# Entry of two retrieval layers: first dots and products ahead of the second tile's norm and queries, and six gather places first

## The chip, the cores and the metric

The kernel runs on one core of one Trainium2 chip. The metric is the device time of one launch in microseconds, as the median of several runs.

## The reference

Two blocks of a transformer work on 256 tokens of width 1024, and a third block (sparse attention, linear attention, mixture of experts) follows. Everything is float32. After its mixer each of the first two blocks runs a product-key retrieval layer, and that is where the change lies. Cut to what matters:

```python
def peer_ffn(h, w_q, sub_keys, down, up):        # h: 256 tokens in blocks of 128
    q = (xb @ w_q).reshape(n, 8, 2, 128)         # 8 heads, 2 halves of a key
    s = einsum('thpk,pnk->thpn', q, sub_keys)    # 128 scores for each half
    s_top, i_top = top_k(s, 16)
    best_s, best_pos = top_k(all 16 x 16 sums, 16)
    idx = ...                                    # 16 experts for each head: 128 picks a token
    gate = softmax(best_s)
    act = gelu(einsum('thkd,td->thk', down[idx], xb))
    return einsum('thk,thkd->td', gate * act, up[idx])

x = x + g1 * mixer(...)
h2 = rms_norm(x, norm2_g) * (1 + sc2) + sh2
x = x + g2 * peer_ffn(h2, ...)
```

Each token picks 128 experts out of 16384. Each expert is a row of 1024 numbers to be dotted with the token and another row of 1024 to be added to the output.

## The kernel before

The tokens are two tiles of 128 (NT), a token to a partition. The two expert rows lie side by side in HBM, 8 KB for an expert. One gather is one indirect DMA issued by POOL (line 676): it brings pick n of all 128 tokens of a tile, 1 MB, into a gather place. A layer has 256 gathers, 128 for each tile. There are eight places (GSLOTS): 0 to 3 lie in the arena, 4 to 7 in two slots of the weight ring that the layer borrows. Places 4 and 5 need the mixer's output weights to be used up (semaphore pout1), places 6 and 7 the first chunk of the query weights, which both tiles use (semaphore pq).

Two picks make a group, here called a round j, of which a layer has 128 (GROUPS). For each round DVE makes two dots, one a gather (down, line 1423), each a fused multiply and sum over 1024 columns. ACT applies gelu and the gate and turns the two results into two diagonal matrices (weigh, lines 885 to 894). PE multiplies these with the second halves of the two gathered rows and accumulates in PSUM (line 2278, "the up product"), and then increments up_used. POOL, which waits for up_used, then issues the gathers that reuse the two places. So a place is taken from the issue of a gather to the end of its round's product.

The picks of the next heads are worked out among all this. PE makes a query step s in four quarters of eight matmuls each (quarter; L1921), then scores(s) (L2231); ACT copies both out (query_out, score_out); DVE runs top-k in 15 steps (top_k) between dots. A step s is a chunk of four key halves for one tile, in the order QUERY; step 0 is done in two half steps (first_query, first_scores), so that head 0's picks come early. The tables QUARTERS and QUERIED say after which rounds j the quarters and scores of steps 3 to 7 stand. All orders are written out by hand, one program for each engine. In layer 0 the order around the entry is this.

- DVE: norm of tile 0, top-k of head 0 (which releases gather 0), residual of tile 1 (add_tile(1)), norm of tile 1 (start(1)), then the dots with top-k steps between them.
- PE: transposes and first query halves of tile 0, last projection of the mixer, step 1 and its scores, transposes of tile 1 (turn(1)), step 2 and its scores, then the rounds.
- ACT: copies for these, then the sum of squares and root of tile 1 (enter(1)), then its copies, then the rounds.
- POOL: gathers 0 to 3, 4 and 5 (pout1), 6 and 7 (pq of step 2), then two after each round.

In layer 1 the norm of tile 1 comes before the top-k of head 0 in both kernels. SP loads the query weights of chunk 3 (wq0_last, wq1_last) once the slot of chunk 1 is free, that is after step 3, and two rows of modulation weights after steps 6 and 7; each of these loads is 2 MB.

Of the kernel before, what the change touches and what calls it, by code (L numbers as in the profile page):

```python
# [22 lines left out]
NT = T // P  # L23
# [7 lines left out]
PICKS = 128  # L31
GSLOTS = 8
# [90 lines left out]


QUERY = [(0, 0), (1, 0), (0, 1), (1, 1), (2, 0), (3, 0), (2, 1), (3, 1)]
QUARTERS = {3 * (i // 2) + i % 2: (3 + i // 4, i % 4) for i in range(20)}
QUERIED = {j: s for j, (s, k) in QUARTERS.items() if k == 3}


def selections(l, m, head=1):  # L130
# [4 lines left out]
PER = 2  # L135
GROUPS = PICKS * NT // PER


def slot_free(l, n):

    return GROUPS * l + (n - GSLOTS) // PER + 1


def operand(tag, n):
# [64 lines left out]
def program(nc, a, out):  # L209

    ctx = ExitStack()
    with ctx:
# [10 lines left out]
        S = Sems()  # L223
# [130 lines left out]
        turn = list(range(RING))  # L354
# [91 lines left out]

        def gslot(l, n):

            k = n % GSLOTS
            if k < 4:  # L450
                return G_arena[:, k]
            return ring[:, lent[l][(k - 4) // 2], 2 * D * (k % 2):2 * D * (k % 2) + 2 * D]

        def wait_gathered(eng, l, n):
            eng.wait_ge(S[f"gathered{n % GSLOTS}"], 16 * ((PICKS * NT * l + n) // GSLOTS + 1))

        g_landed = [S[f"g_landed{i}"] for i in range(2)]

# [17 lines left out]
        place = mo(NT, 34)  # L476
# [179 lines left out]
        @block.gpsimd  # L656
        def _(pool):
            for l in range(2):
                for n in range(PICKS * NT):
                    t, at = n // PICKS, n % PICKS  # L660
                    if n == 0:
                        pool.wait_ge(S["idx_ready"], 9 * l + 1)
                    elif n == HEAD:
                        pool.wait_ge(S["idx_ready"], 9 * l + 2)
                    elif n % (2 * HEAD) == 0:
                        pool.wait_ge(S["idx_ready"], 9 * l + n // (2 * HEAD) + 2)
                    if n >= GSLOTS:
                        if n % PER == 0:
                            pool.wait_ge(S["up_used"], slot_free(l, n))
                    elif n == 4 and l == 0:  # L670
                        pool.wait_ge(S["pout1"], 4)
                    elif n == 6:
                        pool.wait_ge(S["pq"], query_no(l, QUERY.index((0, 1))))
                    elif l and n == 0:
                        pool.wait_ge(S["up_used"], GROUPS * l)
                    pool.indirect_dma_start(  # L676
                        out=gslot(l, n), out_offset=None, in_=a["experts"],
                        in_offset=bass.IndirectOffsetOnAxis(ap=idx_all[:, t, at:at + 1], axis=0)).then_inc(
                        S[f"gathered{n % GSLOTS}"], 16)


        @block.scalar
        def _(act_):
# [142 lines left out]
            def peer(l):  # L826
# [42 lines left out]
                head_out(0)  # L869
                head_out(1)  # L870
                gate_out(0, 0)
                query_out(1)
                score_out(1)
                if l == 0:
                    enter(1)
                turned_out(2)
                turned_out(3)
                query_out(2)
                score_out(2)

                def weigh(j):
                    t, at = PER * j // PICKS, PER * j % PICKS
# [14 lines left out]
                for j in range(GROUPS):  # L897
                    g, i = j // 8, j % 8
                    weigh(j)
                    if j - 1 in QUERIED:  # L900
                        query_out(QUERIED[j - 1])
                    if j - 3 in QUERIED:
                        score_out(QUERIED[j - 3])
                    if j == 4:
                        gate_out(0)
                    if j == 10 or (j % HEAD == 8 and HEAD < j < 7 * HEAD):
                        gate_out(j // HEAD + 1)
                    if i == 5 and g in TOTALS[l]:
                        mod_total_out(TOTALS[l][g])
                    if l == 0 and (g, i) == (11, 0):  # L910
                        act_.wait_ge(S["x_peer"], 1)
                        tile_sum(x, h, 0)
                    if l == 0 and (g, i) == (13, 0):
                        tile_root("n1_1", 0)
# [184 lines left out]
        def _(v):  # L1099
# [257 lines left out]
            def peer(l):  # L1357
                def start(t):
                    v.wait_ge(S["x_mix"], NT * l + t + 1)
                    tile_mean(f"n2_{l}", t)  # L1360
                    tile_norm(f"n2_{l}", t, x, h, mod[:, 4], mod[:, 3])

                add_tile(0, (4, 5) if l == 0 else (0, 1), mod[:, 2], ("pout1", "py_pool")[l], "x_mix")
# [54 lines left out]
                def down(g):  # L1418
                    t, hh = g // 8, g % 8
                    for k in range(HEAD):  # L1420
                        row = gslot(l, HEAD * g + k)[:, 0:D]
                        wait_gathered(v, l, HEAD * g + k)
                        ins = v.scalar_tensor_tensor(out=row, in0=row, scalar=1.0, in1=h[:, t], op0=ALU.mult,  # L1423
                                                     op1=ALU.mult, accum_out=act[:, t, HEAD * hh + k:HEAD * hh + k + 1])
                        if k % PER == PER - 1:
                            ins.then_inc(S["down_used"], 1)
                        n = HEAD * (g % 2) + k
                        if g < 2:
                            if n == 0:
                                gates(0, 0, 1)  # L1430
                            for step in (2 * n, 2 * n + 1):
                                if step < STEPS:
                                    top_k(0, step, 1, 2)
                            if n == 12:
                                gates(0, 1, 2)
                            if 0 <= n - 9 < STEPS:
                                top_k(1, n - 9)
                        elif g < BLOCKS - 2 and n % 4 < 3 and n - n // 4 < STEPS:
                            top_k(g // 2 + 1, n - n // 4)
                        if g < BLOCKS - 2 and n == 24:  # L1440
                            gates(g // 2 + 1)
# [12 lines left out]
                if l == 0:  # L1454
                    v.wait_ge(S["modp"], 4 + ROWS)
                    v.tensor_tensor(mrows1, bank[7][:, :], mbias, ALU.add).then_inc(S["rows_made"], 1)
                    add_tile(1, (2, 3), mod[:, 2], "pout1", "x_mix")
                    start(1)
                for g in range(BLOCKS):
                    down(g)  # L1460
                    if g == SHADOW - 1:
# [449 lines left out]
        def _(pe):  # L1911
# [289 lines left out]
            def peer(l):  # L2201
# [57 lines left out]
                for k in range(4):  # L2259
                    quarter(1, k)  # L2260
                scores(1)
                turn(1)
                for k in range(4):
                    quarter(2, k)
                scores(2)

                for j in range(GROUPS):
                    g, i = j // 8, j % 8
# [6 lines left out]
                    for k in range(PER):  # L2275
                        row = gslot(l, PER * j + k)[:, D:2 * D]
                        for c in range(2):
                            ins = pe.matmul(bank[2 * t + c][:, :], diag[:, PER * (j % 2) + k], row[:, 512 * c:512 * c + 512],  # L2278
                                            start=j % (GROUPS // NT) == 0 and k == 0,
                                            stop=(j + 1) % (GROUPS // NT) == 0 and k == PER - 1, skip_group_check=True)  # L2280
                    ins.then_inc(S["up_used"], 1)
                    if j - 1 in QUERIED:
                        scores(QUERIED[j - 1])
                    if j in QUARTERS:
                        quarter(*QUARTERS[j])
                    if (g, i) == (SHADOW, 7):
                        pe.wait_ge(S["cB"], 5 + l)
                        pe.wait_ge(S["pq_ev"], query_no(l, 7))
# [437 lines left out]
```

## Time and profile before

| | |
|---|---|
| median of 3 runs | 2444.6 us (2443.27 to 2445.58) |
| profiled execution, its own time | 2443.39 us |
| its span, first to last instruction | 2441.5 us |
| mean granted TensorE clock | 0.97 |
| PE busy, share of the span | 2078.7 us, 85% |
| DVE busy | 1158.2 us, 47% |
| 512 gathers | 536.90 MB, 53.3% of the 16 DMA engines' span |

The span is cut into 40 slices of 61 us. The retrieval layers run from about 230 to 925 us and from about 967 to 1640 us. A share of busy time over the whole span says little about an entry that lasts 60 us; windows and timelines of the two entries are needed.

### The profile page before, as it was taken

To read this page: it belongs to the slowest core of one execution; us is meant where nothing else is said; L and a number is where in the kernel's file an instruction comes from. 1 tells how busy PE (TensorE), PEld (TensorE's weight loads), DVE (VectorE), ACT (ScalarE), POOL (GpSimd) and SP (SyncE) were. 2 spreads that over 40 slices of the span, in tenths; PEclk is the share of its full clock that TensorE was granted. 3 is DMA by queue.
4 is the path that set the end of the run, shared out by engine and by line. 5 is a ranking of instruction groups with operands and counts; after the bars stand their busy time and mean duration, and the time that the engine had idled before them with its cause. 6 is when DMAs were issued, how large, how long until landed. Compare 5 with 4: busy or idle time off the path is not lost. (4 is left out here: it accounts for less than half of the span.)

```text
span 2441.5 us, 21439 instructions
## 1 busy us (share of the span) xinstructions
PE 2078.7 (85%) x7589; PEld 987.9 (40%) x7589; DVE 1158.2 (47%) x2844; ACT 647.2 (27%) x1815; POOL 599.2 (25%) x516
## 2 busy tenths in 40 slices
PE   7999899777777778898777777778999899999998
PEld 2455555232323336554223222224445444444443
DVE  2333675666676555675776667443524311111111
ACT  2232333323332322333323333222341110010011
POOL 0000343444444440343444444430000000000000
PEclk8999899999999999999999999999999899999999
DMA  8595799999999994999999999985321479999996
GB/s 351 206 381 219 282 420 421 421 421 419 412 416 417 414 420 172 386 419 421 421 418 419 412 420 421 408 344 229 157 110 57 191 303 427 426 428 427 428 426 266
DMA packets 98909, 864.05 MB, mean 354 GB/s; under 512 B 11352, under 2 KB 11480, under 8 KB 13552
## 3 DMA queue, kind: packets, MB, share of 16 engines
q0 software_dynamic: 73728, 536.90, 53.3%
q1 hardware_dynamic: 25072, 325.75, 32.1%
q8 instruction: 62, 1.02, 0.2%
q14 instruction: 47, 0.39, 0.0%
HBM read 861.56 MB, written 1.05 MB: 353 GB/s over the span
## 5 line engine op out<-in xcount | busy, mean ns | idle before, releaser
L2278 PE MATMUL bank<-ring,arena 128*128 128x512 f32 x1024 | 478.1, 611 | 141.1 <-ACT arena L894 141.0
L2278 PE MATMUL bank<-arena 128*128 128x512 f32 x1024 | 489.2, 623 | 125.8 <-ACT arena L894 125.8
L676 POOL DMA_INDIRECT arena<-in_experts,arena x256 | 299.2, 1169 | 659.3 <-PE bank L2278 332.7
L1423 DVE SCALAR_TENSOR_TENSOR ring<-ring,h 128x1024 f32<-128x1024 f32 x256 | 313.7, 1225 | 266.3 <-DMA ring<-in_experts,arena 265.6
L1423 DVE SCALAR_TENSOR_TENSOR arena<-arena,h 128x1024 f32<-128x1024 f32 x256 | 313.5, 1225 | 208.8 <-DMA arena<-in_experts,arena 207.7
L676 POOL DMA_INDIRECT ring<-in_experts,arena x256 | 299.9, 1171 | 369.3 <-PE bank L2278 301.2
L2278 PEld LDWEIGHTS bank<-ring,arena 128*128 128x128 f32 x1024 | 187.4, 192 | 414.7 <-ACT arena L894 224.4
L2278 PEld LDWEIGHTS bank<-arena 128*128 128x128 f32 x1024 | 191.4, 196 | 402.9 <-ACT arena L894 206.8
L885 ACT ACTIVATE arena<-arena 128x2 f32<-128x2 f32 x256 | 52.0, 203 | 866.0 <-DVE ring L1423 444.2
L1921 PE MATMUL bank<-ring,hT 128*128 128x512 f32 (+2 forms) x608 | 251.8, 571 | 9.2 <-DVE arena L1671 4.8
L2582 PE MATMUL bank<-ring,arena 128*64 128x512 f32 x768 | 223.4, 593 | 2.2 <-ACT arena L1066 1.2
L894 ACT ACTIVATE arena<-const,arena 128x128 f32<-128x128 f32 x512 | 177.6, 394 | 16.6 <-PE bank L2278 8.4
L1921 PEld LDWEIGHTS bank<-ring,hT 128*128 128x128 f32 x608 | 115.6, 193 | 136.5 <-issue 124.4
L1880 DVE TENSOR_TENSOR arena<-arena,bank 128x512 f32<-128x512 f32 x16 | 11.0, 688 | 307.7 <-PE bank L2582 307.7
L1921 PEld LDWEIGHTS bank<-hT,ring 128*128 128x128 f32 x1024 | 125.0, 197 | 25.0 <-issue 22.9
L2582 PEld LDWEIGHTS bank<-ring,arena 128*64 128x64 f32 x768 | 71.7, 137 | 146.2 <-issue 144.8
L1921 PE MATMUL bank<-hT,ring 128*128 128x128 f32 x1024 | 126.2, 280 | 3.1 <-ACT hT L836 3.1
L889 ACT ACTIVATE arena<-arena 128x1 f32<-128x1 f32 x512 | 122.9, 287 | 8.4
L2628 PE MATMUL bank<-ring,arena 128*64 128x512 f32 x256 | 113.3, 595 | 9.1 <-DVE arena L1882 9.1
L2628 PE MATMUL bank<-arena 128*64 128x512 f32 x256 | 113.3, 595 | 0.0
L2582 PE MATMUL bank<-arena 128*64 128x512 f32 x256 | 112.8, 594 | 0.0
L1066 ACT ACTIVATE arena<-bank 128x512 f32<-128x512 f32 x32 | 17.4, 594 | 214.8 <-PE bank L1921 214.8
(434 smaller groups left out, 1713.5 us busy)
## 6 DMA issues: line engine op xcount, KB each, us to landing
ring<-in_w_gate SPq DMA_DIRECT2D x32, 2048.0 KB, 15.0
ring<-in_mod_w SPq DMA_DIRECT2D x24, 2048.0 KB, 11.7
ring<-in_w_up SPq DMA_DIRECT2D x16, 2048.0 KB, 17.0
arena<-in_w_up SPq DMA_DIRECT2D x16, 2048.0 KB, 21.5
ring<-in_w_down SPq DMA_DIRECT2D x16, 2048.0 KB, 11.5
arena<-in_w_down SPq DMA_DIRECT2D x16, 2048.0 KB, 16.0
ring<-in_w_in SPq DMA_DIRECT2D x9, 2048.0 KB, 7.3
ring<-in_peer_w_q SPq DMA_DIRECT2D x8, 2048.0 KB, 12.4
```

The lines of the kernel that those rows point to most:

```text
L676: pool.indirect_dma_start(out=gslot(l, n), out_offset=None, in_=a["experts"], in_offset=bass.IndirectOffsetOnAxis(ap=idx_all[:, t, at:at + ...
L885: link(act_.activation(part, part, ACT.Gelu_apprx_tanh))
L889: ins = act_.activation(act[:, t, k:k + 1], act[:, t, k:k + 1], ACT.Copy, scale=gate[:, t, k:k + 1])
L894: ins = act_.activation(diag[:, PER * (j % 2) + k], ident, ACT.Copy, scale=act[:, t, at + k:at + k + 1])
L1066: act_.activation(xs[:, 4 * half:4 * half + 4].rearrange("p a b -> p (a b)"), bank[half][:, :], ACT.Copy).then_inc(S["x_sel_ev"], 1)
L1423: ins = v.scalar_tensor_tensor(out=row, in0=row, scalar=1.0, in1=h[:, t], op0=ALU.mult, op1=ALU.mult, accum_out=act[:, t, HEAD * hh + k:HE ...
L1880: v.tensor_tensor(hpair.rearrange("p f c -> p (f c)"), flat_sg, bank[3][:, :], ALU.mult).then_inc(S["pair_made"], 1)
L1921: ins = pe.matmul(dst, lhsT, rhs, start=i == 0, stop=i == len(pairs) - 1)
L2278: ins = pe.matmul(bank[2 * t + c][:, :], diag[:, PER * (j % 2) + k], row[:, 512 * c:512 * c + 512], start=j % (GROUPS // NT) == 0 and k == ...
L2582: ins = pe.matmul(bank[2 + j][CAP * k:CAP * k + CAP, :], xs[:, q, CAP * k:CAP * k + CAP], w_k[3 * k + j][:, q], start=q == 0, stop=q == KT ...
L2628: ins = pe.matmul(bank[c][CAP * k:CAP * k + CAP, :], hsel[:, f, CAP * k:CAP * k + CAP], w_k[3 * k + 2][:, f, 512 * c:512 * c + 512], start ...
```

## The change

In layer 0, DVE makes dot 0 right after the residual of tile 1, then the mean for tile 1's norm; the norm itself stands behind dot 1. ACT does tile 1's sum of squares and root ahead of the copy of step 1. In both layers the first up product stands ahead of tile 1's transposes on PE, and step 2 moves into rounds 1 and 2 (two quarters after each product). The quarters of steps 3 to 7 are dealt out again: ten in each 13 rounds from round 3 to round 27, where there were two in each three from round 0 to round 28. The copies on ACT move with them. The first twelve gathers use only places 0 to 5, so gathers 6 to 11 wait for rounds 0 to 2 instead of step 2; gathers 12 and 13 are the first in places 6 and 7 and wait for step 2; from gather 14 on each gather waits for the round that ended eight gathers earlier, as before.

```diff
-QUARTERS = {3 * (i // 2) + i % 2: (3 + i // 4, i % 4) for i in range(20)}
-QUERIED = {j: s for j, (s, k) in QUARTERS.items() if k == 3}
+QUARTERS = {1: [(2, 0), (2, 1)], 2: [(2, 2), (2, 3)]}
+QUARTERS.update({3 + 13 * i // 10: [(3 + i // 4, i % 4)] for i in range(20)})
+QUERIED = {j: parts[-1][0] for j, parts in QUARTERS.items() if parts[-1][1] == 3}
...
+EARLY_SLOTS = 6
+def place_of(n):
+    return n % EARLY_SLOTS if n < 2 * EARLY_SLOTS else (n - EARLY_SLOTS) % GSLOTS
+def users(place, n):
+    return [m for m in range(n) if place_of(m) == place]
 def slot_free(l, n):
-    return GROUPS * l + (n - GSLOTS) // PER + 1
+    return GROUPS * l + users(place_of(n), n)[-1] // PER + 1
...
 # POOL
-                    if n >= GSLOTS:
+                    if users(place_of(n), n):
                         if n % PER == 0:
                             pool.wait_ge(S["up_used"], slot_free(l, n))
                     elif n == 4 and l == 0:
                         pool.wait_ge(S["pout1"], 4)
-                    elif n == 6:
+                    elif n == 2 * EARLY_SLOTS:
                         pool.wait_ge(S["pq"], query_no(l, QUERY.index((0, 1))))
...
 # ACT
                 gate_out(0, 0)
-                query_out(1)
-                score_out(1)
                 if l == 0:
                     enter(1)
-                turned_out(2)
-                turned_out(3)
-                query_out(2)
-                score_out(2)
+                query_out(1)
...
                     weigh(j)
+                    if j == 0:
+                        score_out(1)
+                    if j == 1:
+                        turned_out(2)
+                        turned_out(3)
...
 # DVE
+                        if l == 0 and (g, k) == (0, 0):
+                            tile_mean("n2_0", 1)
+                        if l == 0 and (g, k) == (0, 1):
+                            shifted(1)
...
                     add_tile(1, (2, 3), mod[:, 2], "pout1", "x_mix")
-                    start(1)
...
 # PE
                 scores(1)
-                turn(1)
-                for k in range(4):
-                    quarter(2, k)
-                scores(2)
...
                     ins.then_inc(S["up_used"], 1)
+                    if j == 0:
+                        turn(1)
                     if j - 1 in QUERIED:
                         scores(QUERIED[j - 1])
-                    if j in QUARTERS:
-                        quarter(*QUARTERS[j])
+                    for part in QUARTERS.get(j, ()):
+                        quarter(*part)
```

The first place is PE at the entry of layer 0 in the kernel before, from step 1 and its scores (L2231) to the products of round 3. L2209 is turn(1), L1921 with 128x128 is a query step or one of its quarters (x8), L2278 the up product; two products without anything between them show as x8.

```order
L1921 MATMUL bank<-hT,ring 128x128 x32
L2231 MATMUL bank<-cols,arena 128x128 x4
L2209 MATMUL bank<-const,h 128x128 x8
L1921 MATMUL bank<-hT,ring 128x128 x32
L2231 MATMUL bank<-cols,arena 128x128 x4
L2278 MATMUL bank<-arena 128x512 x4
L1921 MATMUL bank<-hT,ring 128x128 x8
L2278 MATMUL bank<-arena 128x512 x4
L1921 MATMUL bank<-hT,ring 128x128 x8
L2278 MATMUL bank<-ring,arena 128x512 x8
L1921 MATMUL bank<-hT,ring 128x128 x8
L2278 MATMUL bank<-arena 128x512 x4
```

The same place in the changed kernel, where turn(1) is L2230, a query step or a quarter L1942, scores L2252 and the product L2295.

```order
L1942 MATMUL bank<-hT,ring 128x128 x32
L2252 MATMUL bank<-cols,arena 128x128 x4
L2295 MATMUL bank<-arena 128x512 x4
L2230 MATMUL bank<-const,h 128x128 x8
L2295 MATMUL bank<-arena 128x512 x4
L1942 MATMUL bank<-hT,ring 128x128 x16
L2295 MATMUL bank<-ring,arena 128x512 x4
L1942 MATMUL bank<-hT,ring 128x128 x16
L2295 MATMUL bank<-arena 128x512 x4
L2252 MATMUL bank<-cols,arena 128x128 x4
L1942 MATMUL bank<-hT,ring 128x128 x8
L2295 MATMUL bank<-arena 128x512 x4
```

Round 0's product now stands where turn(1) stood, and the 32 matmuls of step 2 follow products 1 and 2 in two halves of 16.

The second place is DVE in layer 0 before the change, from the end of the residual of tile 1 (L1142) to dot 1. L1126 is the mean, L1131 to L1134 the norm of tile 1, L1423 a dot, L1414 to L1416 the gates of head 0, L1157 and L1159 steps of top-k.

```order
L1142 TENSOR_TENSOR x<-x,arena 128x512
L1126 TENSOR_SCALAR stat<-stat 128x1
L1131 RECIPROCAL stat<-stat 128x1
L1132 SCALAR_TENSOR_TENSOR h<-x,stat,arena 128x1024
L1134 TENSOR_TENSOR h<-h,arena 128x1024
L1423 SCALAR_TENSOR_TENSOR arena<-arena,h 128x1024
L1414 TENSOR_REDUCE cols<-arena 128x1
L1415 RECIPROCAL cols<-cols 128x1
L1416 TENSOR_TENSOR arena<-arena,cols 128x16
L1157 MAX cols<-arena 128x8 x2
L1159 MAX_INDEX cols<-cols,arena 128x8 x2
L1423 SCALAR_TENSOR_TENSOR arena<-arena,h 128x1024
```

The same place in the changed kernel: L1157 is the end of the residual, L1441 a dot, L1141 the mean, L1432 to L1434 the gates, L1146 to L1149 the norm.

```order
L1157 TENSOR_TENSOR x<-x,arena 128x512
L1441 SCALAR_TENSOR_TENSOR arena<-arena,h 128x1024
L1141 TENSOR_SCALAR stat<-stat 128x1
L1432 TENSOR_REDUCE cols<-arena 128x1
L1433 RECIPROCAL cols<-cols 128x1
L1434 TENSOR_TENSOR arena<-arena,cols 128x16
L1172 MAX cols<-arena 128x8 x2
L1174 MAX_INDEX cols<-cols,arena 128x8 x2
L1441 SCALAR_TENSOR_TENSOR arena<-arena,h 128x1024
L1146 RECIPROCAL stat<-stat 128x1
L1147 SCALAR_TENSOR_TENSOR h<-x,stat,arena 128x1024
L1149 TENSOR_TENSOR h<-h,arena 128x1024
```

Dot 0 comes first, and the three instructions of the norm come behind dot 1.

The third place is ACT in the changed kernel, layer 0, from the exponential of head 0's gate (L877): L723 and L728 are enter(1), L856 is query_out(1), L895 to L904 one weigh, L870 is score_out(1), L851 the copies of tile 1's transposes. In the kernel before, the two copies of step 1 stood ahead of enter(1), and the copies of the transposes and of step 2 ahead of the first weigh.

```order
L877 ACTIVATE arena<-arena 128x16
L723 ACTIVATE h,stat<-x 128x1024
L728 ACT_TABLE_LOAD
L728 ACTIVATE stat<-stat 128x1
L856 ACTIVATE arena<-bank 128x512
L895 ACT_TABLE_LOAD
L895 ACTIVATE arena<-arena 128x2
L899 ACTIVATE arena<-arena 128x1 x2
L904 ACTIVATE arena<-const,arena 128x128 x2
L870 ACTIVATE arena<-bank 128x512
L895 ACTIVATE arena<-arena 128x2
L899 ACTIVATE arena<-arena 128x1 x2
```

So query_out(1) now waits behind a root that needs DVE's mean, and the first weigh needs neither tile 1's transposes nor step 2.

## Rows read from the trace of the kernel before

Times are microseconds from the start of the span unless a column is marked ns.

**Rows 1.** Windows: stretch, length, busy of each engine, clock, DMA share, GB/s.

```profile
251.50:293.80 42.30, 38.17 (x181) 25.71 (x180) 27.45 (x93) 14.85 (x41) 14.01 (x12) 0.93 0.62 238
293.80:393.80 100.00, 92.93 (x380) 54.35 (x379) 69.63 (x172) 33.94 (x104) 44.08 (x38) 1.00 1.01 421
500.00:900.00 400.00, 309.43 (x679) 122.41 (x679) 259.55 (x588) 126.46 (x418) 186.52 (x158) 0.98 1.01 417
973.00:1014.60 41.60, 37.48 (x183) 24.77 (x183) 31.24 (x104) 14.96 (x41) 14.32 (x14) 0.96 0.94 368
```

**Rows 2.** Timeline of POOL, layer 0: start, length, issue of one gather [idle before].

```profile
229.54 1.07 POOL L676 DMA_INDIRECT arena<-in_experts,arena  x1 [229.09 <-DVE arena L1407]
236.02 0.94 POOL L676 DMA_INDIRECT ring<-in_experts,arena  x1 [0.30 <-issue]
259.88 1.38 POOL L676 DMA_INDIRECT ring<-in_experts,arena  x1 [22.92 <-PE bank L1921]
270.34 1.60 POOL L676 DMA_INDIRECT arena<-in_experts,arena  x1 [7.84 <-PE bank L2278]
284.21 1.31 POOL L676 DMA_INDIRECT ring<-in_experts,arena  x1 [1.00 <-PE bank L2278]
```

**Rows 3.** Line 676, 229 to 237: gathers 0 (the least) to 5 (the most).

```profile
DMA to landing us min/median/max: 9.8/12.4/15.5
```

**Rows 4.** Line 676: 259 to 262 is gathers 6 and 7; 284.1 to 284.3 is gather 14.

```profile
DMA to landing us min/median/max: 6.0/7.1/8.1
DMA to landing us min/median/max: 9.6/9.6/9.6
```

**Rows 5.** Timeline of DVE, layer 0, where line 1423 is a dot.

```profile
233.52 0.74 DVE L1142 TENSOR_TENSOR x<-x,arena 128x512 f32<-128x512 f32 x1
244.91 0.16 DVE L1131 RECIPROCAL stat<-stat 128x1 f32<-128x1 f32 x1 [1.29 <-ACT stat L713]
247.57 1.22 DVE L1423 SCALAR_TENSOR_TENSOR arena<-arena,h 128x1024 f32<-128x1024 f32 x1
250.37 1.23 DVE L1423 SCALAR_TENSOR_TENSOR arena<-arena,h 128x1024 f32<-128x1024 f32 x1
257.09 1.23 DVE L1423 SCALAR_TENSOR_TENSOR ring<-ring,h 128x1024 f32<-128x1024 f32 x1
```

**Rows 6.** Timeline of ACT, layer 0.

```profile
242.22 1.05 ACT L708 ACTIVATE h<-x 128x1024 f32<-128x1024 f32 x1
263.40 0.20 ACT L885 ACTIVATE arena<-arena 128x2 f32<-128x2 f32 x1
```

**Rows 7.** Timeline of PE, layer 0: L2209 transposes, L1921 queries, L2231 scores, L2278 products.

```profile
247.71 1.97 PE L2209 MATMUL bank<-const,h 128*128 128x128 f32 x8 [6.01 <-DVE h L1134]
264.89 5.17 PE L2278 MATMUL bank<-arena 128*128 128x512 f32 x8 [3.44 <-ACT arena L894]
269.90 1.95 PE L1921 MATMUL bank<-hT,ring 128*128 128x128 f32 x16
285.56 3.60 PE L2278 MATMUL bank<-arena 128*128 128x512 f32 x8
288.99 1.95 PE L1921 MATMUL bank<-hT,ring 128*128 128x128 f32 x16
290.78 3.60 PE L2278 MATMUL bank<-arena 128*128 128x512 f32 x8
```

**Rows 8.** Timelines of DVE and POOL, layer 1.

```profile
976.44 1.22 DVE L1423 SCALAR_TENSOR_TENSOR arena<-arena,h 128x1024 f32<-128x1024 f32 x1 [0.61 <-DMA arena<-in_experts,arena]
973.68 1.41 POOL L676 DMA_INDIRECT ring<-in_experts,arena  x1 [0.30 <-issue]
1004.41 0.93 POOL L676 DMA_INDIRECT ring<-in_experts,arena  x1 [1.26 <-PE bank L2278]
```

**Rows 9.** Line 676, layer 1: gathers 0 (least) to 5 (most); gather 14.

```profile
DMA to landing us min/median/max: 5.5/9.8/13.3
DMA to landing us min/median/max: 10.2/10.2/10.2
```

More of the change, by code:

```diff
@@ L447, in gslot @@
         def gslot(l, n):
-            k = n % GSLOTS
+            k = place_of(n)
             if k < 4:
@@ L454, in wait_gathered @@
         def wait_gathered(eng, l, n):
-            eng.wait_ge(S[f"gathered{n % GSLOTS}"], 16 * ((PICKS * NT * l + n) // GSLOTS + 1))
+            k = place_of(n)
+            eng.wait_ge(S[f"gathered{k}"], 16 * (l * len(users(k, PICKS * NT)) + len(users(k, n)) + 1))
         g_landed = [S[f"g_landed{i}"] for i in range(2)]
@@ L678, in _ @@
                         in_offset=bass.IndirectOffsetOnAxis(ap=idx_all[:, t, at:at + 1], axis=0)).then_inc(
-                        S[f"gathered{n % GSLOTS}"], 16)
+                        S[f"gathered{place_of(n)}"], 16)
         @block.scalar
@@ L1360, in start, with shifted @@
                     tile_mean(f"n2_{l}", t)
+                    shifted(t)
+                def shifted(t):
                     tile_norm(f"n2_{l}", t, x, h, mod[:, 4], mod[:, 3])
```

## The prediction

> **What bounds the kernel now.** The windows come first, because a share over the whole span hides an entry of 60 us. In the body of layer 0 (500 to 900 us) the 16 DMA engines are busy 1.01 of the time at 417 GB/s, while PE is busy 309 of 400 us and DVE 260; in the 100 us after the entry they move 421 GB/s, and there PE too is busy for 93 us, which will matter below [rows 1]. So the transfers set the pace: a gather of 1.049 MB every 2.49 us at 421 GB/s, 4.98 us a round. With that, a retrieval layer ends when its last gather has landed, and what can be won in it is the time at its entry in which the DMA engines have nothing to do.
>
> Next come the issues on POOL and their times to landing. Gathers 0 to 5 of layer 0 are issued from 229.54 to 236.02 and land from 239.3 (229.54 + 9.8) to 251.5 (236.02 + 15.5) [rows 2, 3]. Gather 6 is issued only at 259.88, after 22.92 us of waiting for step 2 of the queries, and lands 6.0 us later, at 265.9; gather 7 lands at 269.7 [rows 2, 4]. Gather 14, issued at 284.21, lands at 293.8 [rows 2, 4]. Between 251.5 and 293.8 nine gathers land, which take 9 x 2.49 = 22.4 us; so 19.9 of these 42.3 us are lost to the DMA, and their window shows 238 GB/s [rows 1]. In layer 1 gather 0 lands at 973.0 and gather 14 at 1014.6 (1004.41 + 10.2) [rows 8, 9]: 41.6 us for 14 gathers, 34.9 us, so only 6.7 are lost, and the window shows 368 GB/s [rows 1]. That is the most that each entry can give.
>
> Last, why the gathers are late. DVE ends the residual of tile 1 at 234.3, but dot 0 starts at 247.57 [rows 5], 8 us after gather 0 has landed, because the norm of tile 1 stands in front and waits for ACT. The first product starts at 264.89 [rows 7], 1.49 after its gelu [rows 6], which stood behind the copies of step 2. All six places are held until then.
>
> **The change in layer 0, step by step.** Dot 0 starts when gather 0 is there: 239.5. From dot 0 to dot 1 it was 2.80 us [rows 5]; the mean adds 0.15, so dot 1 runs from 242.4 to 243.7. The norm of tile 1 costs 2.66 on DVE (244.91 to 247.57 [rows 5]) and now stands behind dot 1; the three steps from 250.37 to 257.09 are 2.24 each [rows 5], so dot 2 starts at 247.3, dot 3 ends at 250.8 and dot 5 at 255.3. All six gathers have landed before their dots from dot 2 on. ACT's sum of squares (1.05 [rows 6]) is done by 236; its root waits for DVE's mean behind dot 0, until 241. That is the one wait added: queued behind it on ACT is the copy of step 1, and behind that PE's scores of step 1. They go 1.3 us later; the first weigh needs dot 1 only at 243.7, so this costs nothing. Without that cover it would be the same 1.3 us.
>
> Product 0 starts 1.5 us after dot 1: 245.2. PE's clock was low after a similar pause and the product took 5.0 us to the next piece (264.89 to 269.90), against 3.43 at full speed (285.56 to 288.99) [rows 7]; I take 5.0, so it ends at 250.2. Tile 1's transposes (1.97 after a pause [rows 7]) follow and end before product 1 can start, at 252.3. It ends at 255.7. Half of step 2, two quarters of 1.79 (288.99 to 290.78 [rows 7]), follows until 259.3; product 2 until 262.8; the other half until 266.4; product 3 until 269.8. POOL issues 0.4 us behind the end of a product (269.90 to 270.34 [rows 2, 7]).
>
> So gathers 6 and 7 are issued at 250.6 and land at 256.6 and 260.4: where the DMA has run dry, the first of a pair takes 6.0, and the pair 269.7 - 259.88 = 9.8 [rows 2, 4]. Gathers 8 and 9 are issued at 256.1 and follow at 262.9 and 265.4. Gathers 10 and 11 are issued at 263.2; the DMA is dry for a moment and they land at 269.2 and 273.0. Gathers 12 and 13 (issued 266.8, after step 2) land at 275.5 and 278.0, and gather 14 (issued 270.2) at 280.5. Before it was 293.8: **a lead of 13.3 us**, of 19.9 that were lost. Six places instead of eight cost nothing in this stretch, as before gathers 6 and 7 came later than any round would have allowed.
>
> **Does the lead hold?** From round 3 PE has 3.43 for each product, 1.79 x 10/13 for quarters, and some 0.9 for scores once in five rounds: 3.43 + 1.38 + 0.18 = 4.99 us a round, against the DMA's 4.98. Before it was two quarters in three rounds, 4.80. PE starts round 4 at 272.5 (round 3's end, scores, a quarter), some 4 us after its dots allow (gather 9 at 265.4 + 1.3 + 1.5 = 268.2). That backlog neither grows nor shrinks, and the DMA has six gathers (14.9 us) in the queue to cover it: landing, dot, weigh, product, issue and start take 1.3 + 1.5 + 3.4 + 0.4 + 3.5 = 10.1, so 4.8 us are to spare. It is tight, but each 2 MB load of SP in this stretch gives PE 5 us more. I take no loss; the bound is in the rivals.
>
> **Layer 1.** Its norm of tile 1 is not moved. Gather 1's dot ends at 977.7 [rows 8], so product 0 starts at 979.2 instead of 985.08, after a pause of 8.6 us in which step 2 used to run: PE has nothing to fill it now. Here are the two ends. At full speed product 0 ends at 982.6, product 1 (dot 3 ended at 983.3) at 988.2, step 2 and product 2 at 995.2, product 3 at 1002.2, and gather 14 lands at 1012.8: a gain of 1.8. If product 0 and the transposes run at 1.2 GHz all through (7.0 and 2.0 us), gathers 6 and 7 come after the six first ones have landed (987.0 = 973.68 + 13.3 [rows 8, 9]), and gather 14 lands at about 1016.6: a loss of 2. The product before, after a pause of 3.4 us, lay between; I take the middle, **0**.
>
> **Sum.** 13.3 + 0 = 13.3 us. The profiled execution took 2443.39, which gives 2430.1; the median is 1.2 above it, so 2431.3. The chip's other work is the same in amount, and the layer's later parts all hang on its last gather.
>
> **Two rules of the Trainium skill.** A gather that finds the DMA dry landed 6.0 us after its issue [rows 4]. The page "DMA: Bandwidth & Descriptors", section "Anatomy of one DMA — SWDGE (gpsimd) path", puts a fixed cost of about 2.0 us beside the bytes over 436 GB/s: by it 1.049 MB would be there after an estimated 4.4 us, and the holes ahead of gathers 6 and 10 would shrink by 1.6 us each, for some 2428. The trace doesn't agree, so the row stands. The other speaks against the change: "TensorE: Matmul & The Clock Gate", section "Loop structure matters more than you think", warns that a wait for DMA between matmuls sends the array back to half clock. The rows show that clock in the product at 264.89; the rival on the clock below is priced from them.
>
> **The rivals.** (1) *The clock stays low.* With product 0 at 7.0 us and the transposes at 2.0 in layer 0, product 1 starts at 254.2 and all that follows 1.9 later; with the loss of 2 in layer 1 the gain is 9.4: 2435.2. For it: a pause in both layers. Against: in layer 0 PE's pauses are short, two of about 2 us. (2) *The other side: the rounds become PE's.* A product that starts after a wait, with a quarter behind it, may take more than 4.98 + its share; the records themselves read 3.60 and 1.95 [rows 7], that is 5.3 to 5.4 a round with 10/13 quarters and the scores, if nothing overlapped. 0.35 to 0.45 us a round for 25 rounds in both layers is 17.5 to 22.5 us, more than the lead: 2449 to 2454. It decides from a mean round of 5.25 us (13.3/50 above 4.98), and makes the kernel slower by over 0.2% from 5.35. Against: starts 3.43 and 1.79 apart, and SP's loads. Half of it, a lead worn down by 7 us, gives 2438. (3) *The change does nothing*, because the layer doesn't end with its transfers, or gathers 0 to 5 land later for a reason outside. Then 2444. Against: 1.01 for 400 us [rows 1]. (4) *Quick restarts and a full clock in both entries*: 13.3 + 1.8 + some 2: 2427.5.
>
> **How the numbers follow.** Forecast (2428.5 to 2433.5) 0.60, rival 4 0.10, rival 1 0.12, rival 2 in its mild form 0.08 and in its strong form 0.04, rival 3 0.06. The range from 2426 to 2438.5 leaves out the strong form, most of rival 3 and the edge of the others, under 2 in 10. A measurement of this kernel tells about 0.2%, 4.9 us: faster is all below 2439.7, 0.89; the same 0.07; slower 0.04.
>
> **What the profile after would show.** Dot 0 near 239.5; product 0 near 245; gather 6 issued at 250 to 252 after waiting for a product and no longer for a query; gathers 10 and 11 near 263; gather 14 landed near 280 (layer 0) and within 2 us of its old place from gather 0 (layer 1); DMA share 1.0 from 283 to the end of the layer. Wrong would be a window between 285 and 400 with the DMA share below 0.97 and PE without pauses (rival 2), a product 0 that takes 7 us (rival 1), or a first dot that waits past 242.

## The result, and the profile after

The changed kernel takes 2429.98 us (median of 5 runs, 2428.41 to 2432.18) against 2443.27 of the kernel before (5 runs, 2442.17 to 2445.58): ratio 0.9946, 95% interval 0.9932 to 0.9961, so 13.3 us less. The forecast was 2431.3 in 2426.0 to 2438.5, faster. The profiled execution is the slowest of the five, 2432.18 us, with a span of 2430.4.

The windows first: stretch, length, busy time of each engine, clock, DMA share, GB/s. They answer to [rows 1]: the entry of layer 0 from the landing of gather 5 to that of gather 14, the 100 us behind it, the body of layer 0, and layer 1 from gather 0 to gather 14.

```profile
254.20:284.80 30.60, 30.60 (x162) 20.99 (x161) 22.10 (x74) 12.22 (x34) 15.12 (x13) 1.00 0.90 341
284.80:384.80 100.00, 96.27 (x416) 58.70 (x415) 69.45 (x171) 34.49 (x104) 39.54 (x38) 0.98 1.01 421
500.00:900.00 400.00, 307.37 (x677) 121.13 (x676) 259.67 (x589) 126.82 (x420) 187.91 (x158) 0.99 1.01 416
964.70:1004.20 39.50, 33.92 (x158) 22.00 (x159) 31.25 (x104) 14.69 (x43) 15.34 (x14) 0.88 0.96 385
```

The body is the same as before (DMA share 1.01, 416 GB/s), so the transfers still set the pace. The entry of layer 0 lasts 30.6 us where it lasted 42.3.

POOL's issues in layer 0, which answer to [rows 2]: start, length of an issue, and what it waited for.

```profile
232.29 1.08 POOL L691 DMA_INDIRECT arena<-in_experts,arena  x1 [231.84 <-DVE arena L1425]
238.76 0.94 POOL L691 DMA_INDIRECT ring<-in_experts,arena  x1 [0.30 <-issue]
254.68 1.64 POOL L691 DMA_INDIRECT arena<-in_experts,arena  x1 [14.98 <-PE bank L2295]
258.99 0.94 POOL L691 DMA_INDIRECT arena<-in_experts,arena  x1 [0.54 <-PE bank L2295]
265.99 1.69 POOL L691 DMA_INDIRECT ring<-in_experts,arena  x1 [4.83 <-PE bank L2295]
269.56 0.94 POOL L691 DMA_INDIRECT ring<-in_experts,arena  x1 [0.45 <-PE bank L1942]
273.00 0.94 POOL L691 DMA_INDIRECT arena<-in_experts,arena  x1 [1.25 <-PE bank L2295]
```

Gather 6 waits for a product (L2295), no longer for a query. Everything is some 2.75 us later than before up to gather 0 (232.29 against 229.54), though nothing was changed ahead of it; in the thirteen profiles of this study gather 0 is issued between 226.4 and 232.3. So times are read from the issue of gather 0 on: gather 6 after 22.4 us (30.3 before), gather 14 after 40.7 (54.7 before).

How long the issues took to land: gathers 0 to 5 (the least is gather 0, the most gather 5), gathers 6 and 7, 8 and 9, 10 and 11, and gather 14, which answers to [rows 3, 4].

```profile
DMA to landing us min/median/max: 9.7/12.4/15.4
DMA to landing us min/median/max: 7.0/7.3/7.7
DMA to landing us min/median/max: 8.0/8.6/9.3
DMA to landing us min/median/max: 7.6/8.0/8.3
DMA to landing us min/median/max: 11.8/11.8/11.8
```

Gather 5 lands at 254.2 and gather 14 at 284.8. From the issue of gather 0 that is 52.5 us, against 64.3 before: 11.8 us won.

DVE in layer 0, dots (L1441), residual (L1157), mean (L1141) and the first piece of the norm (L1146), which answer to [rows 5].

```profile
236.27 0.73 DVE L1157 TENSOR_TENSOR x<-x,arena 128x512 f32<-128x512 f32 x1
242.03 1.22 DVE L1441 SCALAR_TENSOR_TENSOR arena<-arena,h 128x1024 f32<-128x1024 f32 x1 [5.03 <-DMA arena<-in_experts,arena]
243.18 0.15 DVE L1141 TENSOR_SCALAR stat<-stat 128x1 f32<-128x1 f32 x1
244.91 1.23 DVE L1441 SCALAR_TENSOR_TENSOR arena<-arena,h 128x1024 f32<-128x1024 f32 x1
246.06 0.16 DVE L1146 RECIPROCAL stat<-stat 128x1 f32<-128x1 f32 x1
249.87 1.23 DVE L1441 SCALAR_TENSOR_TENSOR arena<-arena,h 128x1024 f32<-128x1024 f32 x1
256.41 1.23 DVE L1441 SCALAR_TENSOR_TENSOR ring<-ring,h 128x1024 f32<-128x1024 f32 x1
```

DVE now waits 5.03 us for gather 0 ahead of dot 0, and the norm stands behind dot 1. PE in layer 0, products (L2295), scores (L2252), transposes (L2230), queries (L1942), which answer to [rows 7]:

```profile
244.15 1.13 PE L2252 MATMUL bank<-cols,arena 128*128 128x128 f32 x8 [1.57 <-issue]
247.67 6.74 PE L2295 MATMUL bank<-arena 128*128 128x512 f32 x8 [2.39 <-ACT arena L904]
254.24 1.04 PE L2230 MATMUL bank<-const,h 128*128 128x128 f32 x8
255.11 3.60 PE L2295 MATMUL bank<-arena 128*128 128x512 f32 x8
258.55 3.73 PE L1942 MATMUL bank<-hT,ring 128*128 128x128 f32 x32
262.12 3.60 PE L2295 MATMUL bank<-ring,arena 128*128 128x512 f32 x8
275.24 3.60 PE L2295 MATMUL bank<-arena 128*128 128x512 f32 x8
```

Product 0 starts 15.4 us after the issue of gather 0 (35.4 before) and takes 6.74 us against 3.60 for product 1, so it ran almost wholly at the lower of the two clocks, 1.2 GHz: the granted clock from 247.67 to 254.24 is 0.53 of full speed. PE had paused 1.57 and 2.39 us before it. The transposes behind it ran at full speed (1.04 us, granted clock 1.00). PE in layer 1 around product 0, which the forecast put at the end of dot 1 [rows 8] plus 1.5 us:

```profile
961.10 1.16 PE L2252 MATMUL bank<-cols,arena 128*128 128x128 f32 x8 [0.69 <-ACT arena L856]
970.28 5.54 PE L2295 MATMUL bank<-arena 128*128 128x512 f32 x8 [8.03 <-ACT arena L904]
975.66 1.04 PE L2230 MATMUL bank<-const,h 128*128 128x128 f32 x8
976.53 3.60 PE L2295 MATMUL bank<-arena 128*128 128x512 f32 x8
```

PE has nothing to do for 8.03 us there (8.6 were forecast), and its product runs partly at the lower clock (0.65 granted over its 5.3 us).

### The profile page after: what moved, and what is told of

Same layout as the page of the kernel before. It is cut to its first block and busy times, and to the rows that moved or that the text cites. A ratio compares the mean times of both kernels' runs of the same rounds, so it can differ in the third digit from the quotient of the medians.

```text
span 2430.4 us, 21438 instructions
## 1 busy us (share of the span) xinstructions
PE 2076.1 (85%) x7589; PEld 985.4 (41%) x7589; DVE 1157.8 (48%) x2844; ACT 647.2 (27%) x1815; POOL 596.6 (25%) x516
## 5 line engine op out<-in xcount | busy, mean ns | idle before, releaser
L2295 PE MATMUL bank<-arena 128*128 128x512 f32 x1040 | 495.6, 622 | 139.0 <-ACT arena L904 139.0
L2295 PE MATMUL bank<-ring,arena 128*128 128x512 f32 x1008 | 470.3, 610 | 128.9 <-ACT arena L904 128.8
L1441 DVE SCALAR_TENSOR_TENSOR arena<-arena,h 128x1024 f32<-128x1024 f32 x260 | 318.5, 1225 | 240.2 <-DMA arena<-in_experts,arena 239.1
L1441 DVE SCALAR_TENSOR_TENSOR ring<-ring,h 128x1024 f32<-128x1024 f32 x252 | 308.8, 1225 | 232.3 <-DMA ring<-in_experts,arena 231.6
L2295 PEld LDWEIGHTS bank<-arena 128*128 128x128 f32 x1040 | 194.6, 197 | 419.2 <-ACT arena L904 219.8
L2295 PEld LDWEIGHTS bank<-ring,arena 128*128 128x128 f32 x1008 | 183.9, 192 | 397.6 <-ACT arena L904 212.0
L895 ACT ACTIVATE arena<-arena 128x2 f32<-128x2 f32 x256 | 52.1, 203 | 879.7 <-DVE arena L1441 476.0
L1942 PE MATMUL bank<-ring,hT 128*128 128x512 f32 (+2 forms) x608 | 252.2, 572 | 9.1 <-DVE arena L1692 4.8
L904 ACT ACTIVATE arena<-const,arena 128x128 f32<-128x128 f32 x512 | 177.6, 394 | 8.4
L1942 PEld LDWEIGHTS bank<-ring,hT 128*128 128x128 f32 x608 | 115.6, 193 | 136.9 <-issue 124.8
L1942 PEld LDWEIGHTS bank<-hT,ring 128*128 128x128 f32 x1024 | 124.1, 196 | 20.6 <-issue 20.6
L1942 PE MATMUL bank<-hT,ring 128*128 128x128 f32 x1024 | 125.6, 279 | 1.7 <-ACT hT L851 1.7
```

Of the source, the lines that this page charges most:

```text
L895: link(act_.activation(part, part, ACT.Gelu_apprx_tanh))
L904: ins = act_.activation(diag[:, PER * (j % 2) + k], ident, ACT.Copy, scale=act[:, t, at + k:at + k + 1])
L1942: ins = pe.matmul(dst, lhsT, rhs, start=i == 0, stop=i == len(pairs) - 1)
```

## The experiments

Each kernel is compared with the kernel before in runs on the same chip. The cuts of code show only what an experiment changes, shortened; "..." stands for lines left out. "Entry" is the time from the issue of gather 0 to the start of dot 14 on DVE, both read from the timelines: 64.4 us in layer 0 and 47.3 in layer 1 before the change, 52.6 and 45.3 in the changed kernel's profile.

### One layer at a time

```diff
-QUARTERS, QUERIED, place_of(n)             # one table and one rule for both layers
+QUARTERS[l], QUERIED[l], place_of(l, n)    # by layer, as is the order on PE, ACT and DVE
+ORDER = ('new', 'old'); EARLY_SLOTS = (6, 8)   # a: the change in layer 0 alone
+ORDER = ('old', 'new'); EARLY_SLOTS = (8, 6)   # b: the change in layer 1 alone
```

> The change in layer 0 alone; layer 1 keeps the order, the quarters and the eight places of before. Theory of the forecast: layer 0 brings 13.3 us and layer 1 nothing, so 0.9946 of the kernel before, 2430. Theory from the two traces: from the landing of gather 5 to that of gather 14 layer 0 took 42.3 us before and 30.6 after (11.7 won), and layer 1 from gather 0 to gather 14 took 41.6 and 39.5 (2.1 won), so this kernel is at 2443.3 - 11.7 = 2431.6, ratio 0.9952.

> The change in layer 1 alone. Forecast: no gain, 2443.3. From the two traces: 2.1 us, 2441.2, ratio 0.9991. If the two layers add up, the gains of this kernel and of the one with layer 0 alone sum to that of the whole change, 13.3 us.

Layer 0 alone: 0.9954 (0.9938 to 0.9970), 11.2 us less. Layer 1 alone: 1.0002 (0.9993 to 1.0012), nothing. The entry of layer 0 takes 52.1 us in a and 65.3 in b. That of layer 1 takes 46.8 in a (old order) and 46.3 in b (new order). So the gain is that of layer 0. The two gains sum to 10.7 us by the ratios, against 13.3 for the whole change, which is within the intervals. The 2.1 us that the first trace seemed to show in layer 1 was the scatter of one profile: the same program up to round 2 of layer 1 gave 45.3, 46.3, 48.1, 48.1, 46.6 and 47.3 us in the changed kernel and in b, e, h, i and j, a mean of 46.9, against 47.3 and 46.8 with the old order.

### The places by themselves, and the order by itself

```diff
 # c: the new order with eight places from the first gather
-EARLY_SLOTS = 6
+EARLY_SLOTS = (8, 8)     # gather 6 waits for step 2, which now ends behind round 2
 # d: the kernel before, with only the six early places
-    k = n % GSLOTS
+    k = n % 6 if n < 12 else (n - 6) % GSLOTS
```

> The changed kernel with eight places from the first gather: gather 6 waits for step 2 again, and step 2 now ends behind round 2. Theory: POOL issues in order, so gathers 6 and 7 go at 269.6 in layer 0 (254.7 with six places) and at 990.8 in layer 1, and gather 14 lands 12 and 14 us later than in the changed kernel: 2456, ratio 1.005. Rival: the new order alone wins the time and the places don't matter: 2430.

> The kernel before with six places for the first twelve gathers, nothing else. Theory: gather 6 now waits for round 0 instead of step 2, and is issued at 270.3 instead of 259.9 (layer 0) and at 990.5 instead of 980.1 (layer 1); gather 14 lands 4 us later in layer 0 and 3 in layer 1: 2450, ratio 1.003. Rival: the places bring part of the gain by themselves: below 2443.

c: 1.0051 (1.0032 to 1.0070), 2455.95 us; d: 1.0039 (1.0024 to 1.0054), 2454.58. Each half of the change makes the kernel slower alone, and both together make it faster. POOL of c in layer 0:

```profile
232.85 0.94 POOL L695 DMA_INDIRECT ring<-in_experts,arena  x1 [0.30 <-issue]
264.30 0.94 POOL L695 DMA_INDIRECT ring<-in_experts,arena  x1 [30.50 <-PE bank L1956]
282.82 0.94 POOL L695 DMA_INDIRECT ring<-in_experts,arena  x1 [8.18 <-PE bank L2317]
```

Product 0 of c starts at 242.51, 16.1 us after gather 0's issue and so nearly as early as in the changed kernel (15.4), but gather 6 waits 30.50 us for step 2. In layer 1 it is issued at 997.04, 33.2 us after gather 0 (17.1 in the changed kernel). By layer, the new order alone wins nothing in layer 0 (entry 65.1 us, 64.4 before) and all of the loss lies in layer 1 (58.9, 47.3 before). In d gather 6 waits for product 0 and is issued 41.0 us after gather 0 instead of 30.3 in layer 0. Its entry takes 73.8 and 53.4 us, 9.4 and 6.1 more than before, where 4 and 3 were expected. In layer 0 part of that is no loss: SP's 2 MB of query weights, issued at 295.50, now land ahead of gather 14 (304.2), and they have to be moved anyway. From the issue of the first gather to that of the last, the layers take 5.2 and 6.1 us longer than before. So the sign and the mechanism are right, and the cost was put 2 to 5 us too low (ratio 1.003 and 2450 us expected, 1.0039 and 2454.58 measured).

### Where the gain of layer 0 comes from

```diff
 # e: norm of tile 1 ahead of dot 0 on DVE again; ACT as changed
                     add_tile(1, (2, 3), mod[:, 2], "pout1", "x_mix")
+                    start(1)
...
-                        if l == 0 and (g, k) == (0, 0):
-                            tile_mean("n2_0", 1)
-                        if l == 0 and (g, k) == (0, 1):
-                            shifted(1)
 # i: e, and ACT copies step 1 and its scores ahead of enter(1) again
+                query_out(1)
+                score_out(1)
                 if l == 0:
                     enter(1)
-                query_out(1)
```

> The changed kernel, but the mean and norm of tile 1 stand ahead of dot 0 on DVE again (layer 0); ACT still does its sum and root ahead of the copy of step 1. Theory: DVE is idle for 5.03 us before dot 0 in the changed kernel, waiting for gather 0 (landed 242.0), and with ACT's part first the norm would be done at 242.4; so dot 1 ends 0.3 us later, dots 2 to 5 2.3 earlier, and the time stays: 2430, ratio 0.9946. Rival: it is putting the norm behind the first dots that brings the gain; then product 0 and gather 6 come 3 to 8 us later and the ratio is 0.996 to 0.998.

> The changed kernel, but in layer 0 DVE makes mean and norm of tile 1 ahead of dot 0 and ACT copies step 1 and its scores ahead of tile 1's sum and root, both as before the change; what stays of the change is the order on PE and the six places. Theory: dot 0 starts 8 us after gather 0 has landed again (247.6), product 0 at about 253, and each of the gathers 6 to 14 is issued about 5 us later than in the changed kernel: from the issue of gather 0 to dot 14 it is 58 us (64.4 before, 52.6 in the changed kernel); 2435, ratio 0.997. Rival: the first gathers' data or the clock hides it, and it stays at 0.9946.

e: 0.9950 (0.9932 to 0.9968), entry 52.1 us; i: 0.9964 (0.9950 to 0.9978), entry 59.5. DVE of e in layer 0: the mean for tile 1's norm, and dots 0 and 1.

```profile
237.41 0.15 DVE L1155 TENSOR_SCALAR stat<-stat 128x1 f32<-128x1 f32 x1 [1.29 <-ACT h L727]
241.51 1.22 DVE L1455 SCALAR_TENSOR_TENSOR arena<-arena,h 128x1024 f32<-128x1024 f32 x1
244.31 1.23 DVE L1455 SCALAR_TENSOR_TENSOR arena<-arena,h 128x1024 f32<-128x1024 f32 x1
```

There is no wait ahead of dot 0, which starts 10.1 us after gather 0's issue (9.7 in the changed kernel): the norm fits into the time in which DVE would wait for gather 0. So moving the norm behind dot 1 on DVE brings nothing by itself; what it needed was that ACT made the sum and root of tile 1 early, ahead of the copy of step 1. In i, with ACT's old order, the sum starts at 242.07, dot 0 at 247.41, and product 0 late:

```profile
241.58 0.60 ACT L874 ACTIVATE arena<-bank 128x512 f32<-128x512 f32 x1 [1.27 <-PE bank L2263]
242.07 1.05 ACT L727 ACTIVATE h<-x 128x1024 f32<-128x1024 f32 x1
```

```profile
252.98 6.07 PE L2314 MATMUL bank<-arena 128*128 128x512 f32 x8 [11.45 <-ACT arena L918]
```

Its median is 8.0 us below that of the kernel before (2435.86 against 2443.86); in its profile, of an execution of 2439.9, the entry is 4.9 us shorter than before and 6.9 longer than in the changed kernel (58 were expected, 59.5 measured). So by the entries of single profiles, of the 11.8 us won the order on PE with the six places makes 4.9, and the rest, 6.9, comes with the early dot 0. By the medians the first part is 8 to 9 us and the second 4 to 6. Both parts are real; how large each is stays open, as the same program of layer 0 gave entries of 50.7 to 53.5 us (the changed kernel, a, f and j). e and i differ in ACT's order alone, and that is 7.4 us of entry.

### Clock and pauses before product 0

```diff
 # f: in layer 1, transposes of tile 1 and two quarters of step 2 ahead of round 0
 # g: filler matmuls behind scores(1): 2 in layer 0, 9 in layer 1
+                for _ in range(FILL[l]):
+                    pe.matmul(bank[0][:, :], ones, cst("causal"), start=True, stop=True)
 # k: f in layer 1, and 2 and 4 fillers
+                if l == 1:
+                    turn(1)
+                    for k in range(2):
+                        quarter(2, k)
                 for j in range(GROUPS):
```

> The changed kernel, but in layer 1 the transposes of tile 1 and two of the four quarters of step 2 run ahead of round 0's product, in PE's pause of 8.0 us there. Theory: the pause shrinks, product 0 runs at a higher clock (5.54 us in the changed kernel), PE is 3.6 us ahead from round 1, and gather 14 lands 1.8 us earlier against gather 0 (37.7 instead of 39.5): 2428, ratio 0.9938. Rival: the DMA sets the pace here and nothing changes: 39.5.

> The changed kernel with filler matmuls (into a bank that product 0 overwrites) behind the scores of step 1: 2 in layer 0 (1.7 us), 9 in layer 1 (7.7 us), so that the array is at work in the pause before product 0. It adds work that the reference has not. Theory of the clock: product 0 takes 3.5 us instead of 6.74 and 5.54, gathers 6 and 7 are issued 3 us (layer 0) and 2 us (layer 1) earlier, and gather 14 lands 1 to 2 us earlier in each layer: 2427, ratio 0.9935. Rival: the clock at product 0 doesn't matter, since product 1 waits for dot 3 anyway: 2430, ratio 0.9946.

> The changed kernel with half of step 2 ahead of round 0 in layer 1 and filler matmuls in PE's pauses (2 in layer 0, 4 in layer 1). It adds work that the reference has not. Theory: 1 to 2 us less in each layer than the changed kernel, ratio 0.993 (2426). Rival: what gathers 6 and 7 win, gathers 10 to 14 give back, because they wait for the products behind step 2, and the ratio is that of the changed kernel.

> The changed kernel once more, beside the next one on the same chip. Both theories: ratio 0.9946 +- 0.0015, and in layer 1 from the issue of gather 0 to dot 14 a value between 45.3 and 48.1 us, which is what three profiles of the same layer 1 program have shown so far (45.3, 48.1, 48.1).

| kernel | ratio, 95% interval | entry, layer 0 | layer 1 |
|---|---|---|---|
| changed | 0.9946 (0.9932 to 0.9961) | 52.6 | 45.3 |
| j, changed again | 0.9937 (0.9924 to 0.9949) | 53.5 | 47.3 |
| f | 0.9938 (0.9919 to 0.9957) | 50.7 | 46.4 |
| g | 0.9938 (0.9920 to 0.9956) | 52.1 | 45.9 |
| k | 0.9944 (0.9931 to 0.9957) | 54.2 | 45.6 |

None can be told from the changed kernel. In g the clock did what the theory said. PE of g in layer 0, fillers (L2298), product 0 and 1:

```profile
244.44 1.88 PE L2298 MATMUL bank<-const 128*128 128x512 f32 x4
247.00 3.70 PE L2317 MATMUL bank<-arena 128*128 128x512 f32 x8 [0.67 <-ACT arena L918]
250.53 1.04 PE L2244 MATMUL bank<-const,h 128*128 128x128 f32 x8
254.23 3.70 PE L2317 MATMUL bank<-arena 128*128 128x512 f32 x8 [2.66 <-ACT arena L918]
```

Product 0 takes 3.70 us instead of 6.74 (granted clock 1.00 instead of 0.53), and gather 6 is issued 19.5 us after gather 0 instead of 22.4. But product 1 waits 2.66 us for ACT, that is for dot 3, and starts where it would have started. Gather 10 is issued after 33.7 us, exactly as in the changed kernel, and gather 14 after 40.7, again as there. What gathers 6 and 7 win is given back. That holds for layer 0.

k has the same program as g in layer 0, and there its product 1 was the slow one:

```profile
251.81 6.76 PE L2317 MATMUL bank<-arena 128*128 128x512 f32 x8 [2.66 <-ACT arena L918]
```

PE waited the same 2.66 us ahead of it, but the granted clock was 0.54 from then until 258.5, where g's product 1 took 3.70 us. Gather 10 went 36.3 us after gather 0 instead of 33.7, and the entry of 54.2 us is the longest in the table. So the fillers do not keep the clock up from execution to execution; they can move the slow product to a place where nothing covers it.

e and g also show that two limits meet at product 1. In g it waits for dot 3, with PE free. In e dot 3 is early (17.5 us after gather 0's issue, 19.8 in the changed kernel), and product 1 starts after 22.8 us all the same, as product 0 took 6.38. No run has both an early dot 3 and a fast product 0; from e's dot 3 and g's product 0 an estimate is that product 1 could start some 2.5 us earlier.

In layer 1 gather 14 is issued 35.0 us after gather 0 in g and 34.5 in f, against 35.4 to 37.6 in the changed kernel and in b, e, h, i and j, and 36.1 in k: 1 to 2 us at best, below what the times can tell.

### The forecast's margin: quarters in every round

```diff
-QUARTERS.update({3 + 13 * i // 10: [(3 + i // 4, i % 4)] for i in range(20)})
+QUARTERS.update({3 + i: [(3 + i // 4, i % 4)] for i in range(20)})
```

> The changed kernel with the 20 quarters of steps 3 to 7 one in each of rounds 3 to 22, instead of ten in each 13 rounds. It tests the forecast's margin: a round takes PE 3.43 + 1.79 + 0.22 = 5.44 us against 4.98 of the DMA. Theory: PE's backlog of 4 us at round 4 grows by 0.46 us a round for 19 rounds, less 5 us for the weight load of SP, to 8 us; 4.8 us are covered, so about 3 us are lost in each layer: 2436, ratio 0.997, with a DMA share below 1 somewhere between 330 and 400 us. Rival: the queue covers it and the time stays at 2430.

0.9964 (0.9951 to 0.9976), 2434.77 us: 4 to 7 us slower than the changed kernel by the ratios of its two series (the interval overlaps that of the first and lies just clear of that of j). Windows of h in layer 0, then the same stretches of the changed kernel:

```profile
320.00:340.00 20.00, 20.00 (x91) 12.35 (x90) 12.67 (x36) 6.47 (x22) 7.28 (x7) 1.00 1.00 402
340.00:360.00 20.00, 20.00 (x101) 13.30 (x100) 14.08 (x38) 6.26 (x22) 9.08 (x8) 1.00 1.00 403
360.00:380.00 20.00, 19.10 (x91) 12.22 (x90) 8.79 (x24) 4.22 (x16) 6.85 (x7) 1.00 1.00 412
```

```profile
320.00:340.00 20.00, 20.00 (x89) 12.33 (x89) 11.72 (x29) 6.59 (x22) 8.19 (x8) 1.00 1.01 422
340.00:360.00 20.00, 19.97 (x89) 12.32 (x89) 14.47 (x44) 5.49 (x20) 8.18 (x8) 1.00 1.01 417
360.00:380.00 20.00, 20.00 (x86) 11.83 (x85) 15.08 (x35) 5.98 (x20) 9.47 (x8) 1.00 1.01 419
```

PE has no pause from 320 to 360 and the DMA falls to 402 and 403 GB/s, against 422 and 417: with the third stretch (412 against 419) 2 us of transfer are lost in this layer. The changed kernel's PE has no pause there either (59.97 us of 60), but its rounds still keep up with the DMA. Layer 1 of h has the same pattern; the changed kernel moves 421 and 420 GB/s in these two stretches:

```profile
1040.00:1060.00 20.00, 20.00 (x90) 12.35 (x90) 12.83 (x37) 6.49 (x22) 8.03 (x7) 1.00 1.00 396
1060.00:1080.00 20.00, 20.00 (x101) 13.30 (x101) 13.28 (x35) 6.18 (x22) 9.31 (x8) 1.00 1.00 404
```

The DMA share stays at 1.00 there, not below 1 as expected; only the GB/s tell. From the first gather's issue to the last one's, h's two layers take 666.2 and 660.9 us, 3.0 more in sum than the changed kernel's 667.4 and 656.7, but 1.0 less than the 669.6 and 658.4 of j, which is the same program as the changed kernel. So the medians and the rates show a loss, and whole layers in single profiles scatter too much to show where it stays. The forecast's rival of a layer paced by PE begins to show one step further: ten quarters in 13 rounds are covered, and with 13 in 13 the DMA is held back for a while.

## Why the prediction was right, point by point

**The bound.** Right: the body of the layer kept its pace, and 11.8 us won at the entry of layer 0 show almost whole at its end. The last gather is issued 667.4 us after gather 0 there, 678.9 before.

**Steps of layer 0.** From the issue of gather 0 the forecast had dot 0 at 10.0 us (measured 9.7), product 0 at 15.7 (15.4), gather 6 at 21.1 (22.4), gather 8 at 26.6 (26.7), gather 10 at 33.7 (33.7), gather 12 at 37.3 (37.3), gather 14 at 40.7 (40.7). The term that was off by size is the landing: gather 14 came 52.5 us after gather 0's issue, not 51.0. Gather 6 took 7.0 us to land, not 6.0, and was issued 1.3 late, but most of that was made up: gather 12 landed after 46.5 us, 46.0 were forecast. The other 1.0 came at gather 13, which landed 3.5 us behind gather 12 (dots 12 and 13 start at 278.86 and 282.36, each as soon as its data is there; the steady rate is 2.49 us); why is open. Nor is the first landing a fixed price: in a, the same program in layer 0, gather 6 took 5.6 us, and gather 14 still landed after 51.9. The lead is 11.8 us instead of 13.3.

**Product 0's clock.** I took 5.0 us; it was 6.74 in the first profile and 6.4 to 6.8 in a, e, f, h and j, which is near the rival's 7.0. It cost nothing further: product 1 was forecast at 252.3 for dot 3, which hid it (255.11 in the profile, 252.4 with the 2.75 us of shift taken off). It did cost gather 6 its 1.3 us. The rival on the clock was right on the product and wrong in its price, as it let all that follows come 1.9 us later: it had the transposes at 2.0 us, and they took 1.04, so product 1 started as forecast. There was nothing to spare: dot 3 alone would have let product 1 start at nearly the same time, which is what g shows.

**The wait added on ACT.** The copy of step 1 went at 243.47, 11.2 us after gather 0's issue; it was 10.3 before. It cost nothing, as forecast. But the forecast had not seen that DVE's part of the move was idle, which e shows: the 5 us of waiting ahead of dot 0 would have held the norm's 2.66.

**Six places.** That they "cost nothing in this stretch" was too weak: without them the changed kernel is 12.5 us slower than the one before (c). They are what lets gather 6 go before step 2.

**Layer 1.** 0 was forecast between a gain of 1.8 and a loss of 2, and 0 it is (b: 1.0002).

**Does the lead hold.** Yes, with a DMA share of 1.01 and 421 GB/s from 284.8 to 384.8. The price of a round held too: with the product at 275.24, the quarter behind it at 278.68 and the next product at 280.46, the starts are 3.44 and 1.78 us apart (3.43 and 1.79 forecast). h shows how near the limit was.

**Restarts.** The Trainium skill's page "DMA: Bandwidth & Descriptors", section "Anatomy of one DMA — SWDGE (gpsimd) path", gave an estimated 4.4 us for a gather on idle queues. The trace doesn't agree: gather 6, which found the queues idle, took 7.0 us, 2.6 more than by the page, and 5.6 in a. Gather 10 took 7.6, but gather 9 was still in flight when it was issued (265.99, landed at 269.5), so it was no such restart, though the forecast counted it as one.

**The sum.** 11.8 + 0 by the traces, 13.3 by the medians with an interval of 9.5 to 16.6 us, 15.4 by the ratio of the second series (j: 12.5 to 18.6). That the medians give the very 13.3 us of the forecast is luck, as its lead was 1.5 us too large. What of the difference is more than scatter stays open; the start of gather 0, ahead of all that was changed, alone moves by 6 us from profile to profile.

## What to carry to other kernels

In a stage whose body is bound by transfers, look at its entry alone and write down for each buffer which event frees it first: here a buffer freed by a later piece of work (step 2) stood in an in-order queue ahead of ones that a product could free, and neither reordering the work nor changing the buffers helped without the other. Follow each new order to the instruction that is late next: a faster product 0 was worth nothing while dot 3 came last (g), and an earlier dot 3 nothing while product 0 was slow (e). When a program's start scatters by some microseconds, measure a change from an event behind the scatter.

## What was unexpected of the hardware

A gather of 1.049 MB that found the DMA queues idle took 5.5 (gather 0 of layer 1 before [rows 9]) to 7.0 us to land; gather 6 of one and the same layer 0 program took 7.0 us in one profile and 5.6 in another (a). Its successor in the pair followed later than the 2.49 us of the steady rate: 3.8 us for gather 7 before [rows 2, 4], 2.6 after. A DMA stage can lose 5% of its rate (402 GB/s instead of 422) while its busy share still reads 1.00. And the same pause of 2.66 us on PE, in the same order of work, left the granted clock at 1.00 in one execution (g) and was followed by a product at 0.54 in another (k).
